# A decoder layer with expert retrieval: the attention projection in two passes of 128 tokens

## The chip, the core and the metric

The kernel runs on one core of one Trainium2 chip. The core has five engines that run side by side, each with its own queue of instructions: PE (TensorE, matrix products), DVE (VectorE), ACT (ScalarE), POOL (GpSimd) and SP (SyncE, which here only issues transfers). The engines order their work by semaphores. Transfers are carried out by 16 DMA engines. The metric is the device time of one execution in microseconds (us).

## What is computed

256 tokens of width 1024 go through two sub-layers, all in float32. The reference, cut:

```python
def token_mixer(h, ...):
    ...
    attn = nsa_attention(...)            # 16 heads, (256, 1024)
    y_a = attn @ w_attn_out
    y_b = conformer_conv(glu_in, ...) @ w_conv_out
    g_a, g_b = jnp.split(g_merge, 2, axis=-1)
    y = jax.nn.sigmoid(g_a) * y_a + jax.nn.sigmoid(g_b) * y_b
    return y @ w_out

def peer_ffn(h, w_q, sub_keys, u, v):
    q = (hf @ w_q).reshape(T, PEER_HEADS, 2, PEER_DQ // 2)     # 8 heads
    s = jnp.einsum('thcd,hckd->thck', q, sub_keys)
    s1, i1 = lax.top_k(s[:, :, 0], 16); s2, i2 = lax.top_k(s[:, :, 1], 16)
    # the best 16 of the 256 sums of pairs: 16 experts per token and head
    ...
        act = jax.nn.gelu(jnp.einsum('cd,ced->ce', hc, u[ec]))
        coef = act * wc
        return jnp.einsum('ce,ced->cd', coef, v[ec])
```

Between the two sub-layers stand a norm of the output, the residual sum and another norm (adaLN-conditioned); after the second one more norm and residual sum.

## The kernel before

**Stages.** Modulation and input projection (until about 250 us), the compressed, selected and window attention head by head (until 375 us), then the stages that the change touches, and from about 440 us the experts. Channels are in tiles of 128 (DT = 8 of them), tokens in TT = 2 halves of 128, called t = 0 and t = 1.

**Weights.** 103 tiles of 512 KB (128 x 1024) come in one order, `w_stream`. SP loads tile n into the place `SLOT[n]` of `ring`, eight places, when the tile that was there before (`PRIOR[n]`) is used up (semaphore `ring_used`, L367). T_AO (tiles 71 to 78) are the attention projection, T_OUT (79 to 86) the output projection, T_WQ (87 to 102) the query projection of the experts, one tile for each of 16 half heads.

**From attention to experts.** PE runs eight `column_tile`s of T_AO over all 256 tokens (L664), each of 8 products of 128x128 by 128x256; DVE multiplies each by its gate and adds the convolution branch into `y` (L1187, L1188, semaphore `v_m`). Then PE runs `out_part(0, k)` for the first tokens' output projection (L726), four of the eight `out_part(1, k)`, `h2_transposes(0)`, the first two query columns and their scores, the other four `out_part(1, k)`, two more query columns and `h2_transposes(1)`. A product of float32 shows as two MATMUL records of PE.
`out_norm(t)` and `ffn_norm(t)` on ACT and `token_norms(t)` on DVE make h2, the input of the experts, which `h2_transposes` and `h2_out` turn into h2T.

**Queries and scores.** `STEPS` lists which half head is projected for which tokens: 20 steps, the first eight for 128 tokens each. `query_columns(i)` and `subkey_scores(i)` run on PE, `query_out` and `score_out` on ACT. The first EARLY = 10 steps stand ahead of the experts; the other ten run between the chunks, one for every two.

**Retrieval.** `retrieve(k, part)` on DVE (three parts) finds for one head and 128 tokens the 16 experts, and gives their indices (`v_idx`). There are 16 units; each covers four chunks. Units 0 and 1 are done ahead of chunk 0, unit k + 2 in the course of unit k.

**Gathers.** POOL fetches for each n of 256 one row of 8 KB (u and v of an expert) for each of 128 tokens, 1 MB, into buffer `PLACE[n]` (L441 to L457). It waits first for all merges (`v_m`), then for the indices of each unit, and for a few buffers for their former content (`OUT_FREE`, `QUERY_FREE`). Twelve buffers are used until gather LATE = 92, from then on 16. Gather n waits until PE has used the row that was in its buffer (`p_row_used`). Four buffers are pairs of ring places; six are the arena.

**Chunks.** A chunk is four rows: DVE takes the dot product of each u with h2 (L1303), ACT the gelu, DVE multiplies by the softmax weight (`cf`), ACT writes four diagonal matrices (L926), and PE adds diagonal times v into PSUM (L697, 16 MATMUL records of 512 columns for a chunk). 64 chunks, 32 for each half of the tokens. `softmax_sum(k)` on DVE needs the exponential of unit k (`unit_exp`, ACT), with which goes a load of ACT's table, and another for the gelu behind it.

## Time and profile before

| | us |
|---|---|
| median of three runs | 1116.71 |
| lowest, highest | 1113.67, 1119.34 |
| profiled execution, its own time | 1119.28 |
| its span, first to last instruction | 1117.5 |
| busy in the span: PE / DVE / ACT / POOL | 966.3 / 728.0 / 280.1 / 328.3 |
| moved by DMA | 363.46 MB |
| of it gathers and other transfers of POOL (software queue) | 292.59 MB |
| mean granted clock of TensorE | 0.949 of 2.4 GHz |

The page's slices are each one fortieth of the span, 27.9 us; a digit is the busy share in tenths. In the rows below, times count from the start of the span. An entry such as "[3.65 <-ACT sig L926]" says that the engine was idle for 3.65 us before, and what ended it. Where a row is for several instructions (x16), its time is that from the first one's start to the last one's end.

### The profile page before, as it was taken

To read this page: it belongs to the slowest core of one execution; us is meant where nothing else is said; L and a number is where in the kernel's file an instruction comes from. 1 tells how busy PE (TensorE), PEld (TensorE's weight loads), DVE (VectorE), ACT (ScalarE), POOL (GpSimd) and SP (SyncE) were. 2 spreads that over 40 slices of the span, in tenths; PEclk is the share of its full clock that TensorE was granted. 3 is DMA by queue.
4 is the path that set the end of the run, shared out by engine and by line. 5 is a ranking of instruction groups with operands and counts; after the bars stand their busy time and mean duration, and the time that the engine had idled before them with its cause. 6 is when DMAs were issued, how large, how long until landed. Compare 5 with 4: busy or idle time off the path is not lost.

```text
span 1117.5 us, 10659 instructions
## 1 busy us (share of the span) xinstructions
PE 966.3 (86%) x3151; PEld 572.7 (51%) x3151; DVE 728.0 (65%) x1901; ACT 280.1 (25%) x770; POOL 328.3 (29%) x324
## 2 busy tenths in 40 slices
PE   5999999998999998899898987878768677878776
PEld 4888888776544765655454543333323233323332
DVE  6698997714455116686676676777677668667553
ACT  2111122143456102413212212221241221221212
POOL 0101002030000001355343445445434444445410
PEclk9999999997899999899899998989999999999988
DMA  9967649883101525999999999999999999999991
GB/s 364 403 245 242 230 154 398 337 237 80 38 20 36 176 90 169 419 422 420 424 421 424 422 423 423 422 422 424 422 423 424 422 423 423 423 422 423 424 422 71
DMA packets 63559, 363.46 MB, mean 325 GB/s; under 512 B 7515, under 2 KB 8171, under 8 KB 30476
## 3 DMA queue, kind: packets, MB, share of 16 engines
q0 software_dynamic: 43136, 292.59, 64.2%
q1 hardware_dynamic: 20364, 70.18, 17.2%
q8 instruction: 26, 0.43, 0.2%
q14 instruction: 33, 0.27, 0.1%
HBM read 361.15 MB, written 1.59 MB: 325 GB/s over the span
## 4 chain that ended last, share of the span: by engine, by line
PE 53%; DMA 35%; DVE 6%; ACT 2%; POOL 2%; issue 2%; SPq 0%; ACTq 0%; DVEq 0%; POOLq 0%
DMA pair<-in_peer_uv,idx 28%; PE pb L484 23%; PE pb L697 16%; DMA ring<-in_peer_uv,idx 4%; PE pb L499 3%; PE pb L635 2%; DMA arena<-in_peer_uv,idx 2%; PE pb L606 2%; PE pb L515 1%; PE pb L676 1%; DVE pair L1303 1%; PE pb L722 1%; PE pb L630 1%; POOL hT L454 1%; PE pb L588 1%
## 5 line engine op out<-in xcount | busy, mean ns | idle before, releaser
L697 PE MATMUL pb<-arena,sig 128*128 128x512 f32 x432 | 212.3, 645 | 63.2 <-ACT sig L926 63.0
L454 POOL DMA_INDIRECT arena<-in_peer_uv,idx x108 | 127.5, 1180 | 234.3 <-PE pb L697 164.6
L484 PE MATMUL pb<-hT,ring 128*128 128x256 f32 x880 | 190.7, 379 | 0.5 <-ACT arena L781 0.5
L484 PEld LDWEIGHTS pb<-hT,ring 128*128 128x128 f32 x880 | 167.0, 190 | 25.1 <-ACT arena L781 1.7
L1303 DVE CUSTOM_DVE_ANT_0 arena<-arena,sig 128x1024 f32<-128x1024 f32 x108 | 130.9, 1227 | 74.2 <-DMA arena<-in_peer_uv,idx 73.5
L697 PEld LDWEIGHTS pb<-arena,sig 128*128 128x128 f32 x432 | 86.4, 206 | 179.7 <-issue 179.4
L923 ACT ACTIVATE gl<-dot 128x4 f32<-128x4 f32 (+1 forms) x67 | 13.7, 205 | 443.9 <-DVE dot L1303 419.4
L697 PE MATMUL pb<-ring,sig 128*128 128x512 f32 x224 | 106.1, 618 | 21.2 <-ACT sig L926 21.2
L1050 DVE SCALAR_TENSOR_TENSOR y<-arena,cols,y x240 | 95.2, 473 | 0.0
L1303 DVE CUSTOM_DVE_ANT_0 ring<-ring,sig 128x1024 f32<-128x1024 f32 x56 | 67.8, 1224 | 29.8 <-DMA ring<-in_peer_uv,idx 29.4
L926 ACT ACTIVATE sig<-ident,cf 128x128 f32<-128x128 f32 x256 | 82.1, 390 | 15.4 <-DVE cf L1307 15.4
L697 PEld LDWEIGHTS pb<-ring,sig 128*128 128x128 f32 x224 | 43.6, 198 | 80.7 <-issue 80.7
L454 POOL DMA_INDIRECT ring<-in_peer_uv,idx x56 | 60.3, 1076 | 65.6 <-PE pb L697 51.7
L697 PE MATMUL pb<-qk,sig 128*128 128x512 f32 x156 | 75.5, 619 | 0.0
L697 PE MATMUL pb<-spare,sig 128*128 128x512 f32 x68 | 43.1, 767 | 32.4 <-ACT sig L926 32.4
L414 POOL DMA_DIRECT2D arena<-in_w_ada x32 | 17.1, 541 | 167.1 <-DVE modst L999 129.4
L1303 DVE CUSTOM_DVE_ANT_0 qk<-qk,sig 128x1024 f32<-128x1024 f32 x39 | 47.8, 1226 | 25.8 <-DMA qk<-in_peer_uv,idx 25.8
L697 PEld LDWEIGHTS pb<-qk,sig 128*128 128x128 f32 x156 | 32.1, 206 | 43.2 <-issue 43.2
L454 POOL DMA_INDIRECT qk<-in_peer_uv,idx x39 | 45.4, 1164 | 20.9 <-PE pb L697 14.8
L999 DVE CUSTOM_DVE_ANT_0 arena<-arena,sc 128x1024 f32<-128x1024 f32 x32 | 37.8, 1222 | 9.1 <-DMA arena<-in_w_ada 8.5
L484 PE MATMUL pb<-qk,ring 128*128 128x256 f32 x192 | 43.4, 379 | 0.0
L484 PEld LDWEIGHTS pb<-qk,ring 128*128 128x128 f32 x192 | 36.3, 190 | 9.1 <-issue 4.8
(226 smaller groups left out, 1220.5 us busy)
## 6 DMA issues: line engine op xcount, KB each, us to landing
ring<-in_w_stream SPq DMA_DIRECT2D x103, 512.0 KB, 6.8
arena<-in_w_ada POOLq DMA_DIRECT2D x32, 512.0 KB, 11.4
arena<-in_w_ada SPq DMA_DIRECT2D x12, 512.0 KB, 13.3
arena<-in_w1k SPq DMA_DIRECT2D x8, 512.0 KB, 8.8
sig<-in_w_ada SPq DMA_DIRECT2D x4, 512.0 KB, 15.3
arena<-in_w1v POOLq DMA_DIRECT2D x1, 2048.0 KB, 7.9
arena<-rev_scratch POOLq DMA_DIRECT2D x16, 128.0 KB, 6.6
arena<-in_peer_uv,idx POOLq DMA_INDIRECT x108, 26.7
```

Of the source, the lines that this page charges most:

```text
L414: g.dma_start(adaw[:, k, :], a["w_ada"][i * 8 + k]).then_inc(ada_more[k], 16)
L454: nc.gpsimd.indirect_dma_start(out=rowat[PLACE[n]], out_offset=None, in_=a["peer_uv"], in_offset=bass.IndirectOffsetOnAxis(ap=idx[:, c, e: ...
L484: last = mm(pb[:, bank, 0:SEQ], w[:, k * P:(k + 1) * P], src[:, k, :], start=(k == 0), stop=(k == DT - 1))
L499: last = mm(pb[:, n, 0:SEQ], ring[:, k, n * P:(n + 1) * P], hT[:, k, :], start=(k == 0), stop=(k == DT - 1))
L606: mm(pb[:, n % 2, 0:2 * keys], qT[0:DQK, h, tt * P:(tt + 1) * P], kT[0:DQK, g, 1:3, 0:keys], start=True, stop=True).then_inc(p_s, 1)
L635: last = mm(o, V[:, kb, (b * GROUPS + g) * DV:(b * GROUPS + g + 1) * DV], PT[:, gi % 2, b * (tt + 1) + kb, :], start=False, stop=((b, kb) ...
L697: last = mm(pb[:, 4 + 2 * t + hf, :], diag[:, c % DEEP, e, :], rowat[PLACE[n]][:, D + hf * 512:D + (hf + 1) * 512], start=(i == 0 and e == ...
L923: fn(gl[:, b, lo:hi], dot[:, b, lo:hi], ACT.Gelu_apprx_tanh).then_inc(a_gl, 1)
L926: fn(diag[:, b, s, :], ident[:, :], ACT.Copy, scale=cf[:, b, s:s + 1]).then_inc(a_dg, 1)
L999: V_.tensor_tensor_reduce(out=w[:, s, :], in0=w[:, s, :], in1=cact, scale=1.0, scalar=0.0, op0=ALU.mult, op1=ALU.add, accum_out=modst[:, s ...
L1050: ins = V_.scalar_tensor_tensor(out=y[:, j, :], in0=upad[:, j, k:k + SEQ], scalar=w, in1=y[:, j, :], op0=ALU.mult, op1=ALU.add)
L1303: V_.tensor_tensor_reduce(out=u, in0=u, in1=h2[:, c // CPT, :], scale=1.0, scalar=0.0, op0=ALU.mult, op1=ALU.add, accum_out=dot[:, c % DEE ...
```

## The change

The attention projection is done in two passes, one for each 128 tokens. The first pass, the first tokens' output projection and then four tiles of the second pass follow one another on PE; the other four tiles of the second pass stand behind the first two queries and scores, and the whole output projection of the second tokens behind them. The merges on DVE are split likewise: eight, then `token_norms(0)`, four, `retrieve(0)`, four, `token_norms(1)`. The second retrieval moves behind the dots of chunk 0.

The tiles of the output and query projections get places of their own outside the ring (`tile_at`): eight in the arena, six in spare, qk, V and y. The gather buffers are reordered: the ring and hT come first, then the arena. The first gather waits for `ring_used` to reach T_OUT (second pass used up), gather 5 for all merges, gather 7 for the output projection, gather 11 for the norms. LATE is 84, and the load of rows[3] stands there. h2 and the diagonals change places in `sig`. STEPS has 22 entries: six half heads for the first tokens, then by turns two for the second tokens and two for all; EARLY is 7, and from chunk 0 on there is one step for each chunk.

```diff
-SOON, SLOTS, LATE = 12, 16, 92
-OUT_FREE, QUERY_FREE = 10, 11
-STEPS = [(m, (0,)) for m in range(4)] + [(m, (1,)) for m in range(4)] + [(m, (0, 1)) for m in range(4, 2 * PH)]
+SOON, SLOTS, LATE = 12, 16, 84
+MERGED_FREE, OUT_FREE, NORM_FREE = 5, 7, 11
+STEPS = [(m, (0,)) for m in range(6)]
+for _m in (0, 2, 4):
+    STEPS += [(_m, (1,)), (_m + 1, (1,)), (_m + 6, (0, 1)), (_m + 7, (0, 1))]
+STEPS += [(m, (0, 1)) for m in range(12, 2 * PH)]
-EARLY = 10
+WQ_ORDER = [m for m, ts in STEPS if TT - 1 in ts]
+EARLY = 7
...
-        s = n % RING if m < 0 else (7, 0, 1, 2, 3, 6)[m] if m < 6 else (7, 0, 1, 6)[(m - 6) % 4]
+        s = n % RING if n < T_OUT else RING + n - T_OUT if m < 0 else RING + DT + m % 6
...
+OUT_BANK = (2, 6)
+MERGE_BANK = [0, 1, 4, 5] * 3 + [4, 5] * 2
+MERGE_BANK_BEFORE = [max((q for q in range(n) if MERGE_BANK[q] == MERGE_BANK[n]), default=-1) for n in range(TT * DT)]
...
+        rowat = [ring[:, 2 * i:2 * i + 2, :].rearrange("p a b -> p (a b)") for i in range(4)]
+        rowat += [hT[:, :, :].rearrange("p a b -> p (a b)")]
+        rowat += [arena[:, 2 * i:2 * i + 2, :].rearrange("p a b -> p (a b)") for i in range(6)]
+        rowat += [pair[:, :]]
+        rowat += [spare[:, :], qk[:, 3 * D:5 * D], qk[:, 5 * D:7 * D], qk[:, 0:2 * D]]
+        tile_at = [ring[:, i, :] for i in range(RING)]
+        tile_at += [arena[:, i, :] for i in (8, 9, 10, 11, 4, 5, 6, 7)]
+        tile_at += [spare[:, 0:D], spare[:, D:2 * D], qk[:, 3 * D:4 * D], qk[:, 4 * D:5 * D],
+                    V[:, :, :].rearrange("p a b -> p (a b)"), yf[:, D:2 * D]]
...
# SP
-                sp.wait_ge(ring_used, PRIOR[n] + 1)
-                sp.dma_start(ring[:, SLOT[n], :], a["w_stream"][n]).then_inc(ring_in[SLOT[n]], 16)
+                if PRIOR[n] >= 0:
+                    sp.wait_ge(ring_used, used(PRIOR[n]))
+                if n == T_OUT:
+                    sp.wait_ge(v_mx, 2 * NU)
+                if n == T_OUT + 4:
+                    sp.wait_ge(p_o, GROUPS * TT)
+                if n == T_WQ + 5:
+                    sp.wait_ge(ring_used, T_WQ)
+                sp.dma_start(tile_at[SLOT[n]], a["w_stream"][n]).then_inc(ring_in[SLOT[n]], 16)
...
# POOL
-            g.wait_ge(v_mx, 2 * NU)
-            g.wait_ge(v_m, DT)
+            g.wait_ge(ring_used, T_OUT)
...
+                if n == MERGED_FREE:
+                    g.wait_ge(v_m, TT * DT)
                 if n == OUT_FREE:
                     g.wait_ge(ring_used, T_WQ)
-                if n == QUERY_FREE:
-                    g.wait_ge(ring_used, T_WQ + 5)
+                if n == NORM_FREE:
+                    g.wait_ge(v_h2, TT)
                 if n == LATE:
...
+                    rows_load(3)
...
# PE
+            def attention_out_half(t, j):
+                tile = T_AO + j
+                if t == 0:
+                    pe.wait_ge(ring_in[SLOT[tile]], 16 * TURN[tile])
+                if MERGE_BANK_BEFORE[t * DT + j] >= 0:
+                    pe.wait_ge(v_m, MERGE_BANK_BEFORE[t * DT + j] + 1)
+                for k in range(DT):
+                    last = mm(pb[:, MERGE_BANK[t * DT + j], 0:P], tile_at[SLOT[tile]][:, k * P:(k + 1) * P],
+                              hT[:, k, t * P:(t + 1) * P], start=(k == 0), stop=(k == DT - 1))
+                last.then_inc(ring_used if t else p_ao, 1)
...
             for k in range(DT):
                 last = out_part(0, k)
             last.then_inc(p_out, 1)
-            for k in range(4):
-                out_part(1, k).then_inc(ring_used, 1)
+            pe.wait_ge(a_o, 2 * GROUPS * TT)
+            for j in range(4):
+                attention_out_half(1, j)
             h2_transposes(0)
-            pe.wait_ge(a_h2T, 2)
             pe.wait_ge(sub_in, 16)
+            pe.wait_ge(v_m, DT + 2)
             query_columns(0)
             query_columns(1)
             subkey_scores(0)
             subkey_scores(1)
-            for k in range(4, DT):
+            for j in range(4, DT):
+                attention_out_half(1, j)
+            for k in range(DT):
                 out_part(1, k).then_inc(ring_used, 1)
-            query_columns(2)
-            query_columns(3)
-            subkey_scores(2)
-            subkey_scores(3)
+            for i in range(2, 6):
+                query_columns(i)
+                if i > 2:
+                    subkey_scores(i - 1)
+            subkey_scores(5)
             h2_transposes(1)
             pe.wait_ge(a_h2T, 4)
-            for i in range(4, EARLY):
+            for i in range(6, EARLY):
                 query_columns(i)
-                if i > 4:
-                    subkey_scores(i - 1)
-            subkey_scores(EARLY - 1)
+                subkey_scores(i)
             for c in range(TT * CPT):
                 expert_chunk(c)
-                i = EARLY + c // 2
...
+                if 0 < c and EARLY + c - 1 < len(STEPS):
+                    subkey_scores(EARLY + c - 1)
+                if EARLY + c < len(STEPS):
+                    query_columns(EARLY + c)
...
# ACT, ahead of the chunks
             out_norm(1)
             query_out(2)
+            query_out(3)
             ffn_norm(1)
-            query_out(3)
+            unit_exp(0)
+            gelu_next()
             score_out(2)
+            query_out(4)
             score_out(3)
+            query_out(5)
+            score_out(4)
+            score_out(5)
             h2_out(1)
...
# DVE
             for part in range(3):
                 retrieve(0, part)
+            for j in range(4, DT):
+                merged(1, j)
             token_norms(1)
-            for part in range(3):
-                retrieve(1, part)
             for c in range(TT * CPT):
...
+                if c == 0:
+                    for part in range(3):
+                        retrieve(1, part)
```

## Rows read from the trace of the kernel before

**Rows 1.** The page, DMA busy tenths and GB/s in 40 slices.
```profile
DMA  9967649883101525999999999999999999999991
GB/s 364 403 245 242 230 154 398 337 237 80 38 20 36 176 90 169 419 422 420 424 421 424 422 423 423 422 422 424 422 423 424 422 423 423 423 422 423 424 422 71
```

**Rows 2.** Stretches: length, busy us of each engine, PEclk, DMA share, GB/s.
```profile
440.00:450.00 10.00, 5.38 (x30) 4.60 (x29) 9.27 (x27) 3.25 (x8) 7.52 (x7) 0.74 0.79 287
...
900.00:1080.00 180.00, 136.34 (x281) 56.31 (x281) 119.04 (x286) 38.62 (x106) 80.80 (x70) 0.92 1.01 423
...
1092.00:1100.00 8.00, 5.98 (x7) 2.50 (x8) 4.79 (x10) 2.69 (x9) 0.00 (x0) 0.58 0.17 72
```

**Rows 3.** Timeline of DVE, the last three dots: start, us, instruction, idle before.
```profile
1096.64 1.23 DVE L1303 CUSTOM_DVE_ANT_0 ring<-ring,sig 128x1024 f32<-128x1024 f32 x1 [0.47 <-DMA ring<-in_peer_uv,idx]
...
1099.10 1.23 DVE L1303 CUSTOM_DVE_ANT_0 qk<-qk,sig 128x1024 f32<-128x1024 f32 x1 [0.81 <-DMA qk<-in_peer_uv,idx]
...
1101.56 1.23 DVE L1303 CUSTOM_DVE_ANT_0 qk<-qk,sig 128x1024 f32<-128x1024 f32 x1 [0.80 <-DMA qk<-in_peer_uv,idx]
```

**Rows 4.** Timeline of POOL: the load of rows[3], gathers 0 and 12.
```profile
375.73 0.53 POOL L436 DMA_DIRECT2D V<-rows_scratch  x1 [3.59 <-PE pb L635]
440.66 1.00 POOL L454 DMA_INDIRECT arena<-in_peer_uv,idx  x1 [64.40 <-DVE idx L1256]
...
473.98 0.94 POOL L454 DMA_INDIRECT arena<-in_peer_uv,idx  x1 [11.33 <-PE pb L697]
```

**Rows 5.** Timeline of PE from the attention projection to chunk 3.
```profile
375.36 27.89 PE L484 MATMUL pb<-hT,ring 128*128 128x256 f32 x128
403.09 20.76 PE L676 MATMUL pb<-ring,y 128*128 128x512 f32 x48
424.16 1.09 PE L685 MATMUL pb<-ident,sig 128*128 128x128 f32 x8 [0.31 <-DVE sig L1207]
...
430.52 7.03 PE L676 MATMUL pb<-ring,y 128*128 128x512 f32 x16
...
469.95 9.83 PE L697 MATMUL pb<-arena,sig 128*128 128x512 f32 x16 [3.65 <-ACT sig L926]
...
500.71 7.03 PE L697 MATMUL pb<-arena,sig 128*128 128x512 f32 x16
```

**Rows 6.** Chain of work that ended last: one query tile for 128 tokens.
```profile
453.96 1.79 PE pb L722 x16
```

**Rows 7.** Timeline of DVE: a merge, the first retrieval's start and end, two dots.
```profile
379.19 0.42 DVE L1187 TENSOR_TENSOR pair<-pb,sig 128x256 f32<-128x256 f32 x1 [7.87 <-PE pb L484]
...
431.13 0.48 DVE L1217 MAX8 v<-sc 128x8 f32<-128x128 f32 x2 [7.02 <-ACT sc L931]
...
439.59 0.17 DVE L1256 SCALAR_TENSOR_TENSOR idx<-e 128x16 int32<-128x16 f32 x1
...
465.42 1.22 DVE L1303 CUSTOM_DVE_ANT_0 arena<-arena,sig 128x1024 f32<-128x1024 f32 x1
...
466.57 1.22 DVE L1303 CUSTOM_DVE_ANT_0 arena<-arena,sig 128x1024 f32<-128x1024 f32 x1
```

**Rows 8.** Weight loads issued in 412:440, 441:470, 449:452, 455:460, us to landing.
```profile
ring<-in_w_stream SPq DMA_DIRECT2D x6, 512.0 KB, 3.8
ring<-in_w_stream SPq DMA_DIRECT2D x4, 512.0 KB, 9.3
ring<-in_w_stream SPq DMA_DIRECT2D x1, 512.0 KB, 8.1
ring<-in_w_stream SPq DMA_DIRECT2D x1, 512.0 KB, 11.8
```

**Rows 9.** Timeline of ACT: from the exponential's table load to the gelu's.
```profile
462.05 1.28 ACT L912 ACT_TABLE_LOAD   x1
...
464.87 0.20 ACT L915 ACTIVATE turned<-eps 128x1 f32<-128x1 f32 x1
```

**Rows 10.** Timeline of PE: scores of one step for 256 tokens.
```profile
489.94 0.61 PE L709 MATMUL pb<-qk 128*128 128x128 f32 x4
```

More of the change, by code:

```diff
@@ L126, with used @@
 SLOT, TURN, PRIOR = tile_places()
+def used(n):
+    return n + 1 if n < T_WQ else T_WQ + 1 + WQ_ORDER.index(n - T_WQ)
+OUT_BANK = (2, 6)
+MERGE_BANK = [0, 1, 4, 5] * 3 + [4, 5] * 2
+MERGE_BANK_BEFORE = [max((q for q in range(n) if MERGE_BANK[q] == MERGE_BANK[n]), default=-1) for n in range(TT * DT)]
 def landed(n):
@@ L294, in build @@
                                                   ("x_in", "c_in", "cols_in", "table_in", "onehot_in", "small_in"))
-        ring_in = [sem(f"ring_in{i}") for i in range(RING)]
+        ring_in = [sem(f"ring_in{i}") for i in range(RING + DT + 6)]
+        p_ao = sem("p_ao")
         ada_in = [sem(f"ada_in{i}") for i in range(2 * DT)]
@@ L472, in _ @@
                     last.then_inc(p_xT, 1)
-            def attention_landed(k):
-                return 2 * (GROUPS * TT - 1) + (2 if k >= DT - 2 else 0)
             def column_tile(bank, tile, src, ready=None, count=lambda k: k + 1):
-                w = ring[:, SLOT[tile], :]
+                w = tile_at[SLOT[tile]]
                 pe.wait_ge(ring_in[SLOT[tile]], 16 * TURN[tile])
@@ L708, in subkey_scores @@
                 for t in ts:
-                    last = mm(pb[:, 2 + i % 2, t * NK:(t + 1) * NK], query[:, m % 4, t * P:(t + 1) * P],
+                    last = mm(pb[:, 2 + i % 2, t * NK:(t + 1) * NK], query[:, i % 4, t * P:(t + 1) * P],
                               subk[:, m, :], start=True, stop=True)
@@ L721, in query_columns @@
                 for k in range(DT):
-                    last = mm(pb[:, i % 2, 0:P], ring[:, SLOT[T_WQ + m], k * P:(k + 1) * P],
+                    if k % 4 == 0:
+                        pe.wait_ge(a_h2T, 2 * ts[0] + k // 4 + 1)
+                    last = mm(pb[:, i % 2, 0:P], tile_at[SLOT[T_WQ + m]][:, k * P:(k + 1) * P],
                               h2T[:, k, ts[0] * P:(ts[0] + 1) * P], start=(k == 0), stop=(k == DT - 1))
                 last.then_inc(ring_used if ts[0] else p_q, 1)
+            pe.wait_ge(a_pt, NU)
             for k in range(DT):
@@ L940, in query_out @@
                 else:
-                    act.wait_ge(ring_used, T_WQ + m + 1)
-                fn(query[:, m % 4, ts[0] * P:(ts[-1] + 1) * P], pb[:, i % 2, 0:len(ts) * P], ACT.Copy).then_inc(a_q, 1)
+                    act.wait_ge(ring_used, used(T_WQ + m))
+                fn(query[:, i % 4, ts[0] * P:(ts[-1] + 1) * P], pb[:, i % 2, 0:len(ts) * P], ACT.Copy).then_inc(a_q, 1)
             out_norm(0)
@@ L1209, in token_norms @@
                 dve.wait_ge(v_h2, t + 1)
-            dve.wait_ge(rows_in, 64)
+            dve.wait_ge(rows_in, 48)
             token_norms(0)
+            for j in range(4):
+                merged(1, j)
             def top16(n_rows, src, work, vals, idxs):
@@ L1232, in retrieve @@
                 t, q = divmod(k, CPT // SEG)
+                swork, cand, cwork, oneh = (v[min(k, 1)] for v in (sworks, cands, cworks, onehs))
                 pair = v16[:, :, :].rearrange("p (h c) k -> p h c k", c=2)
```

105 lines of the change are left out of this document (48 added, 57 removed).

## The prediction, made before the changed kernel was run

> **What bounds the kernel now.** I read first the page's line of DMA by slices, because one resource must explain the second half: from slice 16 on, some 447 us, to slice 39 it shows nines and 420 to 425 GB/s without a gap [rows 1]. The stretches agree: 423 GB/s at a share of 1.01 from 900 us to 1080 us, while PE is busy for only 136 of those 180 us [rows 2]. So from the first row gather on, the kernel moves 256 gathers of 1 MB each (128 rows of 8 KB), plus what weights are left, at one fixed rate; one gather costs 2.48 us of it (1.049 MB at 423 GB/s), which is also the spacing of the last dot products, 1096.64 and 1099.10 [rows 3]. What ends last is then the last landing plus a tail of some 16 us.
>
> Hence the time is set by three things: **when the gathers begin**, **how many bytes are left to move then**, and **whether the DMA runs dry later**. Only these three count below. The stretch 440 to 450 moved 2.87 MB, 6.8 us of full rate, so full rate began at 443.2, 2.5 us after the issue of the first gather at 440.66 [rows 2, 4]. A gather n needs its buffer: the first 12 have free ones, each later one waits until PE has used the row 12 places earlier. In the kernel before that margin is thin but holds: the first 12 gathers (29.8 us) and the four weight tiles issued between 441 and 470 (4 x 1.24 us) last until 478.0, and the 13th is issued at 473.98, so its data flow at 476.5 [rows 4, 8]. Chunk 0 of the experts starts on PE at 469.95 [rows 5].
>
> **Part 1: the first tokens' path gets shorter.** Before, PE does the attention projection of all 256 tokens from 375.36 in 27.89 us, 3.49 a tile, then the first tokens' output projection, 32 records of 0.4325 us (20.76/48), until 416.9 [rows 5]. A tile for 128 tokens should cost what a query column tile of 128 tokens costs: 1.79 us [rows 6]. So the first pass takes 8 x 1.79 = 14.3 us and ends at 389.7, and the first output projection (13.84 us) at 403.5: 13.4 us earlier. Its merges on DVE (two operations of 0.42 us at 256 tokens, less at 128) [rows 7] and the weights, for which SP now has free places as soon as the scores end, lie under PE. A tile landed in 3.8 us while the DMA was idle [rows 8], and the last of these 8 is needed at 401.8. The norms to h2 take as before 7.2 us (416.93 to 424.12) [rows 5], until 410.7; the four tiles of the second pass that PE does meanwhile are 4 x 1.79 = 7.2 us, as long, so they cost nothing. Transposes, first two queries and scores: retrieval started 7.0 us after h2 (424.12 to 431.13) [rows 5, 7]; the wait on half of h2T saves 0.4 us, thus 417.3. Retrieval takes 8.6 us (431.13 to 439.76) [rows 7]: **the first indices are there at 426.0, 13.8 us earlier.**
>
> **Part 2: but the gathers don't start then.** POOL now waits until all of the second pass is used (its first buffers are the ring). Tiles 4 and 5 run at 416.9 to 420.5, but tile 6 needs the bank of tile 4, whose merge stands on DVE behind the whole first retrieval: it comes at 426.8. PE is idle for 6.3 us. In this trace an idle PE loses its clock: after 3.65 us idle, 16 records took 9.83 us where 7.03 is usual, and in 440 to 450 the granted clock is 0.74 on average, that is partly at 1.2 GHz [rows 2, 5]. Tiles 6 and 7 therefore take between 3.6 and 7.2 us and end between 430.4 and 434.0. I take 433.0, since the low stretch after 469.95 lasted 6 us (2.9 us were lost at half speed). With 0.4 us to the issue, gather 0 is issued at 433.4 instead of 440.66: **-7.3 us** (ends -6.3 and -9.9). The second output projection, which frees buffers 7 to 10, is queued behind these tiles: it ends at 446.9, where before it ended at 437.5 [rows 5]. That is later, but seven gathers (17.4 us) cover until 453.3.
>
> **Part 3: bytes left.** Before, 6 query tiles were in by the first gather and 10 of 16 were left; now 5 are in (the sixth waits for y), so one tile more: +1.24 us. The broadcast of rows[3], 0.5 MB, was done at 375.73 on an idle DMA [rows 4]; now POOL issues it ahead of gather 84: +1.2 us. Together **+2.5 us**. The DMA rate stays; that the gathers' buffers lie elsewhere costs nothing that a row shows, between -1 and +1 us.
>
> **Part 4: does the DMA run dry?** This term decides. The chain to chunk 0: after 446.9 PE needs the sixth query tile, which is requested only then, behind seven gathers. Such a load landed 8.1 to 11.8 us after its issue when gathers were queued [rows 8], so at 455.0 to 458.7, and PE has nothing else from 453 on. I take 456.5, the lower end, as fewer gathers are queued. Then the query itself (1.8 to 3.6 us, again after an idle PE), two scores, the 8 transposes, the evacuation behind two score evacuations on ACT, and one more query with its score give some 6 us more, and chunk 0 starts on PE at 464.7, after its first row the 13th gather's data flow at 468.6. The two table loads with the exponential between (462.05 to 464.87) [rows 9] now stand ahead of score 2 on ACT, from 453 to 456, under the same wait. The DMA has work from 435.9 for 29.8 us and two tiles, until 468.2: **0.4 us dry**.
>
> Next, the second retrieval (8.6 us) has moved behind chunk 0's dots. DVE does it, then four dots (1.15 us each [rows 7]), then come gelu, coefficient and diagonals (1.1 us): chunk 1 starts 13.9 us after chunk 0, and as PE had been idle for 5 us, its first row takes 3.4 us and not 1.7. From row to row that is 15.6 us, in which the DMA has 4 gathers and a tile, 11.2 us: **4.4 us dry**. Then PE is the pace: a chunk is 6.9 us (16 x 0.4325), and there is one step of query and score with each chunk instead of every other: 3.5 us for 256 tokens, 1.79 for 128, 0.4 for the score [rows 6, 10]. 10.8 us against the DMA's 9.9: chunk 2 adds 2.0 us (the rest of the slow clock in it), chunk 3 0.9. From chunk 4 the steps are short ones and two more tiles are to be loaded; the margin grows back. Sum 7.7 us; from it I take 1 us, since not all 16 DMA engines are equally far, and those behind still have work. **+6.7 us** (ends +2 with a fast clock and an early tile, +12 with a tile at 458.7).
>
> That some engines lag can be seen at the end: 1092 to 1100 shows a share of 0.17, yet DVE still waits for landings until 1101.5 [rows 2, 3]. So the last landing is set by the slowest engine. In the Trainium skill, DMA: Bandwidth & Descriptors (Latency and other measured facts), two of the engines are called usually slower under descriptors from GpSimd; by it the lag would grow evenly over the gathers, and in the first 16 of them would be well under a microsecond, so the sum stays.
>
> The same page (Queues, rings and completion order) says that each engine takes turns between queues packet by packet. By it the sixth query tile would move at about half the rate, some 4.5 us, and not wait for the gathers ahead; chunk 0 would start some 2 us earlier and the sum would be about 0. The trace's 8.1 to 11.8 us speak against it, so I stay with the rows.
>
> **The sum.** -7.3 + 2.5 + 6.7 = +1.9 us. The profiled execution took 1119.28 us at a span of 1117.5, 2.6 above the median of the three runs, 1116.71, which lie between 1113.67 and 1119.34; the difference goes on the median: **1118.5 us**. About 0.5% (5.6 us) is what a measurement can tell from no change.
>
> **The rivals.**
> (A) The early start is kept: the sixth query tile lands early, PE keeps 2.4 GHz and the dry spells are covered. For it: the margin before held with the same 12 buffers, and the DMA is never seen dry. Against: the second retrieval after chunk 0 is 8.6 us that no other work of DVE hides. It gives -7.3 + 2.5 = -4.8, to -7.4 with the earlier end of the second pass: 1109.3 to 1111.9, about 1110.5. Chance 0.22.
> (B) Slower: the sixth query tile. Requested at 446.9 behind seven gathers, it decides from about 457 on: every microsecond later delays chunk 0, with it gather 12, and as the DMA has only 12 buffers' work, the end, one for one. At 458.7 PE has been idle for 5.7 us, the query takes 3.6 us, chunk 0 starts at about 469 and the 13th gather flows at 473: 5 us dry there, 12 in all. -7.3 + 2.5 + 12 = +7.2: 1124. For it: the 11.8 us seen; against: the backlog is shorter here. Chance 0.22.
> (C) The change doesn't move the start: if the wait for the merges and the slow clock push the end of the second pass 3 us beyond its worst end, gathers start at 437 or later, and -3.7 + 2.5 + 6.7 = +5.5: 1122 or more. Chance 0.06.
> The forecast, 1114 to 1121.5, has 0.50.
>
> **The numbers.** Faster by over 0.5% (under 1111.1): most of A and a little of the forecast's lower tail, 0.22. Slower (over 1122.3): B and C, 0.25. Within: 0.53. For 8 in 10 the range must reach into both: 1109.5 to 1126.
>
> **What would show it.** First gather issued at 433 to 434, 7 us earlier, and the first indices at 426; PE idle between about 420.5 and 426.8, the second output projection ending near 447; PE waiting for the weights of the sixth query near 453 to 456; chunk 0 at about 465; DMA slices below full rate between 465 and 510 us, 5 to 8 us in sum; from there to the end 423 GB/s and the tail unchanged. Were the DMA full from 436 us on, A is right. Were it dry beyond chunk 4, the pace of one step to a chunk was costed too low. I would be wrong altogether if the rate of the gathers changed with their new places or a stall showed after gather 84.

## The result

| | before | changed |
|---|---|---|
| median, us | 1115.72 (20 runs) | 1119.51 (20 runs) |
| lowest to highest, us | 1110.68 to 1121.10 | 1114.50 to 1122.92 |
| profiled execution, its span, us | 1119.28, 1117.5 | 1117.12, 1115.4 |

The ratio is 1.0031, with a 95% interval of 1.0016 to 1.0046: about 3.5 us slower, within the 0.5% that was called no change. The two profiled executions stand the other way round, by 2.1 us. That comes mainly from ahead of the change: the attention projection begins at 375.36 in the one [rows 5] and at 370.92 in the other. It varies from one execution to the next: in x11 below, which does the same work up to there as the kernel before, it begins at 371.44. So everything below is counted **from the start of the attention projection**, and by that the last landing comes 3.5 us later in the changed kernel. From the last dot product's start to the end of the span it takes 15.9 us in the one and 14.8 in the other; -4.4 + 3.5 - 1.2 makes the -2.1. What this tail depends on stands in the last section.

The page of the changed kernel, DMA busy tenths and GB/s in 40 slices, which answer to [rows 1]:

```profile
DMA  9967649884102705989999999999999999999992
GB/s 368 403 236 241 238 153 379 333 256 89 38 20 78 300 1 207 389 331 401 422 422 422 422 423 422 422 424 421 423 423 422 423 424 422 422 423 423 422 423 123
```

The slices 12 to 15, counted from 0, have changed (78, 300, 1, 207 GB/s: the weights come early, then nothing, then the gathers), and the slices at full rate are no longer without a gap: 389, 331 and 401 GB/s stand in slices 16 to 18, from 446 to 530 us. The stretches (length, busy us of each engine, PEclk, DMA share, GB/s), as [rows 2]:

```profile
430.00:440.00 10.00, 10.00 (x24) 4.37 (x24) 0.19 (x1) 0.00 (x0) 6.07 (x7) 1.00 0.87 315
...
460.00:470.00 10.00, 8.73 (x30) 4.75 (x31) 8.47 (x36) 3.05 (x9) 3.66 (x4) 1.00 0.91 342
470.00:480.00 10.00, 5.05 (x12) 2.44 (x12) 9.59 (x28) 3.26 (x9) 0.06 (x1) 0.66 0.82 330
480.00:490.00 10.00, 10.00 (x35) 6.00 (x34) 9.56 (x24) 2.15 (x7) 4.57 (x4) 1.00 0.82 319
490.00:500.00 10.00, 10.00 (x36) 6.24 (x35) 8.83 (x24) 2.42 (x9) 4.06 (x4) 1.00 0.95 346
500.00:510.00 10.00, 10.00 (x40) 5.69 (x39) 5.93 (x17) 6.07 (x15) 5.25 (x4) 1.00 0.98 368
510.00:520.00 10.00, 10.00 (x38) 5.46 (x38) 6.23 (x16) 0.74 (x3) 4.87 (x5) 1.00 1.01 422
...
900.00:1080.00 180.00, 139.61 (x287) 57.53 (x286) 120.04 (x287) 38.62 (x106) 82.06 (x70) 0.92 1.01 423
```

Between 460 and 510 us the DMA moves 342, 330, 319, 346 and 368 GB/s instead of 422. Ten us at each come to 0.80 + 0.92 + 1.03 + 0.76 + 0.54 MB too little: **4.1 MB, or 9.6 us at full rate**. 6.2 us of it lie ahead of 482.6 (351 GB/s from 460 to 466, 330 to 470, 385 to 474, 56 from 478 to 482.6, 2.5 us after the issue of the 17th gather), 3.4 us behind. Afterwards all is as before.

The timeline of PE, which answers to [rows 5]: start, us, instructions, idle before.

```profile
370.92 14.56 PE L693 MATMUL pb<-hT,ring 128*128 128x128 f32 x128
385.31 13.90 PE L713 MATMUL pb<-arena,y 128*128 128x512 f32 x32
...
412.33 3.74 PE L693 MATMUL pb<-hT,ring 128*128 128x128 f32 x32
422.37 6.75 PE L693 MATMUL pb<-hT,ring 128*128 128x128 f32 x32 [6.30 <-DVE y L1230]
428.95 13.90 PE L713 MATMUL pb<-arena,y 128*128 128x512 f32 x32
...
451.79 3.22 PE L759 MATMUL pb<-qk,y 128*128 128x128 f32 x16 [3.14 <-ACT qk L980]
...
461.75 7.10 PE L732 MATMUL pb<-ring,sig 128*128 128x512 f32 x16 [1.18 <-ACT sig L964]
...
475.60 3.75 PE L732 MATMUL pb<-hT,sig 128*128 128x512 f32 x4 [4.95 <-ACT sig L964]
...
488.25 5.31 PE L732 MATMUL pb<-arena,sig 128*128 128x512 f32 x12
...
499.01 7.03 PE L732 MATMUL pb<-ring,sig 128*128 128x512 f32 x16
```

To be seen here: the first pass in 14.4 us where all 256 tokens took 27.89 [rows 5]; 6.30 us without work ahead of tiles 6 and 7, which then take 6.75 us for 3.6 us of work; 3.14 us idle ahead of the sixth query; chunk 0 at 461.75; and 4.95 us idle ahead of chunk 1. For the sixth query the row names ACT, whose evacuation of the fifth ends at 451.75. But in the kernel `query_columns(5)` waits only for the fourth evacuation, done by 446.7, and for its weights: issued at 442.88, they landed 8.8 us later, at 451.7. The timeline of POOL, gathers 0, 12 and 16, which answers to [rows 4]:

```profile
429.40 1.01 POOL L484 DMA_INDIRECT ring<-in_peer_uv,idx  x1 [61.70 <-PE pb L693]
...
463.98 0.93 POOL L484 DMA_INDIRECT ring<-in_peer_uv,idx  x1 [12.82 <-PE pb L732]
...
480.12 0.93 POOL L484 DMA_INDIRECT hT<-in_peer_uv,idx  x1 [10.06 <-PE pb L732]
```

And DVE: the first indices; the second norms, which stand behind 13.91 us of idle time; and the last dot.

```profile
421.40 0.18 DVE L1302 SCALAR_TENSOR_TENSOR idx<-e 128x16 int32<-128x16 f32 x1
...
444.10 1.23 DVE L1238 TENSOR_TENSOR sc<-pb,sc 128x1024 f32<-128x1024 f32 x1 [13.91 <-ACT pair L930]
```

```profile
1100.62 1.23 DVE L1350 CUSTOM_DVE_ANT_0 arena<-arena,sig 128x1024 f32<-128x1024 f32 x1 [0.80 <-DMA arena<-in_peer_uv,idx]
```

### The profile page after: what moved, and what is told of

It reads as the page before. It is cut to its first block, busy times and chain, and to the rows that moved or that the text cites. A ratio compares the mean times of both kernels' runs of the same rounds, so it can differ in the third digit from the quotient of the medians.

```text
span 1115.4 us, 11016 instructions
## 1 busy us (share of the span) xinstructions
PE 962.1 (86%) x3311; PEld 575.9 (52%) x3311; DVE 730.9 (66%) x1917; ACT 280.9 (25%) x774; POOL 329.9 (30%) x324
## 4 chain that ended last, share of the span: by engine, by line
PE 51%; DMA 35%; DVE 6%; ACT 2%; SPq 2%; POOL 2%; issue 2%; ACTq 0%; DVEq 0%; POOLq 0%
DMA ring<-in_peer_uv,idx 29%; PE pb L511 20%; PE pb L732 16%; DMA pair<-in_peer_uv,idx 4%; PE pb L693 3%; PE pb L713 2%; PE pb L662 2%; PE pb L633 2%; DMA arena<-in_w_ada 2%; PE pb L759 1%; DVE ring L1350 1%; DMA arena<-in_w1k 1%; POOL ring L484 1%; PE pb L657 1%; PE pb L615 1%
## 5 line engine op out<-in xcount | busy, mean ns | idle before, releaser
L732 PE MATMUL pb<-ring,sig 128*128 128x512 f32 x288 | 143.6, 657 | 32.5 <-ACT sig L964 32.5
L511 PE MATMUL pb<-hT,ring 128*128 128x256 f32 x752 | 162.8, 379 | 0.5 <-ACT arena L819 0.5
L511 PEld LDWEIGHTS pb<-hT,ring 128*128 128x128 f32 x752 | 142.7, 190 | 21.1 <-ACT arena L819 1.7
L484 POOL DMA_INDIRECT ring<-in_peer_uv,idx x72 | 82.5, 1146 | 170.1 <-PE pb L732 102.3
L961 ACT ACTIVATE gl<-dot 128x4 f32<-128x4 f32 (+1 forms) x67 | 13.7, 205 | 425.1 <-DVE dot L1350 425.1
L732 PEld LDWEIGHTS pb<-ring,sig 128*128 128x128 f32 x288 | 59.2, 210 | 113.2 <-issue 113.1
L1350 DVE CUSTOM_DVE_ANT_0 ring<-ring,sig 128x1024 f32<-128x1024 f32 x72 | 87.1, 1228 | 41.2 <-DMA ring<-in_peer_uv,idx 40.7
L1088 DVE SCALAR_TENSOR_TENSOR y<-arena,cols,y x240 | 95.2, 476 | 0.0
L732 PE MATMUL pb<-qk,sig 128*128 128x512 f32 x132 | 59.4, 600 | 0.0
L732 PE MATMUL pb<-hT,sig 128*128 128x512 f32 x72 | 36.6, 632 | 22.9 <-ACT sig L964 22.9
L732 PE MATMUL pb<-spare,sig 128*128 128x512 f32 x44 | 23.8, 666 | 20.5 <-ACT sig L964 20.5
L885 ACT ACTIVATE pair<-pair,nm 128x128 f32<-128x128 f32 (+1 forms) x64 | 28.5, 447 | 40.2 <-DVE nm L1179 40.1
## 6 DMA issues: line engine op xcount, KB each, us to landing
arena<-in_w_ada SPq DMA_DIRECT2D x12, 512.0 KB, 13.4
qk<-in_w_stream SPq DMA_DIRECT2D x6, 512.0 KB, 13.4
```

The lines of the kernel that those rows point to most:

```text
L484: nc.gpsimd.indirect_dma_start(out=rowat[PLACE[n]], out_offset=None, in_=a["peer_uv"], in_offset=bass.IndirectOffsetOnAxis(ap=idx[:, c, e: ...
L511: last = mm(pb[:, bank, 0:SEQ], w[:, k * P:(k + 1) * P], src[:, k, :], start=(k == 0), stop=(k == DT - 1))
L732: last = mm(pb[:, 4 + 2 * t + hf, :], diag[:, c % DEEP, e, :], rowat[PLACE[n]][:, D + hf * 512:D + (hf + 1) * 512], start=(i == 0 and e == ...
L885: fn(S[:, n % 4, b, 0:keys], S[:, n % 4, b, 0:keys], ACT.Exp, scale=-1.0, bias=nm[:, n % 2, b:b + 1], accum_out=Z[:, n % 2, b:b + 1]).then ...
L1088: ins = V_.scalar_tensor_tensor(out=y[:, j, :], in0=upad[:, j, k:k + SEQ], scalar=w, in1=y[:, j, :], op0=ALU.mult, op1=ALU.add)
L1350: V_.tensor_tensor_reduce(out=u, in0=u, in1=h2[:, c // CPT, :], scale=1.0, scalar=0.0, op0=ALU.mult, op1=ALU.add, accum_out=dot[:, c % DEE ...
```

## The experiments

Each kernel was timed against the kernel before in five rounds. All compute the full result. The table counts from the start of the attention projection (in brackets the us in the trace at which that is); "13th" is the issue of the first gather that reuses a buffer, "17th" that of the first one that needs a row of chunk 1, and "last dot" the start of the last dot product, which is the last landing. Three kernels have a buffer more (x4, x8, x11); for them it is the 14th and the 18th gather. x2 and x4 start their gathers 1 us ahead of the changed kernel with the same code up to there: tiles 6 and 7 took 5.76 and 5.82 us in them, behind the same 6.3 us of idle time, where the changed kernel's trace has 6.75. So differences of 1 us in the table are no more than one execution differs from the next.

| kernel | first gather | 13th | 17th | last dot | 17th to last dot | ratio to before, 95% |
|---|---|---|---|---|---|---|
| before (375.36) | 65.3 | 98.6 | 110.4 | 726.2 | 615.8 | 1 |
| changed (370.92) | 58.5 | 93.1 | 109.2 | 729.7 | 620.5 | 1.0031 (1.0016 to 1.0046) |
| x1 retrieval ahead of chunk 0 (371.97) | 58.5 | 100.1 | 110.4 | 731.6 | 621.3 | 1.0037 (1.0019 to 1.0056) |
| x2 sixth tile's own place (372.04) | 57.5 | 88.6 | 104.5 | 724.5 | 620.0 | 0.9993 (0.9973 to 1.0014) |
| x3 more banks (370.62) | 51.5 | 87.9 | 104.1 | 724.4 | 620.4 | 0.9980 (0.9956 to 1.0004) |
| x4 thirteen buffers (373.78) | 57.5 | 94.0 | 109.6 | 726.7 | 617.1 | 1.0003 (0.9980 to 1.0025) |
| x5 idle time used (373.75) | 57.2 | 96.8 | 106.0 | 727.4 | 621.4 | 1.0007 (0.9983 to 1.0030) |
| x6 x5 and x3 (371.41) | 51.5 | 93.5 | 102.6 | 723.7 | 621.1 | 0.9976 (0.9952 to 0.9999) |
| x7 x6 and x2 (371.04) | 51.5 | 86.0 | 95.2 | 716.5 | 621.4 | 0.9912 (0.9880 to 0.9943) |
| x8 x6, thirteen buffers (373.17) | 51.5 | 93.5 | 102.1 | 720.1 | 618.0 | 0.9943 (0.9922 to 0.9963) |
| x9 x5, one line on ACT (374.59) | 57.2 | 91.8 | 101.0 | 722.1 | 621.2 | 0.9958 (0.9939 to 0.9977) |
| x10 x6, one line on ACT (371.67) | 51.5 | 87.8 | 97.0 | 718.0 | 621.0 | 0.9930 (0.9903 to 0.9958) |
| x11 before, thirteen buffers (371.44) | 65.3 | 98.6 | | 725.6 | | 1.0001 (0.9982 to 1.0020) |
| x12 x7 with EARLY 6 (373.87) | 51.5 | 85.0 | 95.0 | 716.7 | 621.7 | 0.9909 (0.9876 to 0.9942) |

The theory was that the end follows the moment at which the first chunks free their buffers, because the DMA runs dry until then; the rivals were that the gathers' start decides, or the bytes and the new places. **The sixth column carries the answer**: in the changed kernel and its nine relatives with twelve buffers, the last landing comes 620.0 to 621.7 us after the issue of the 17th gather, while the first gather's issue varies by 7 us and the 17th's by 15. And the last dot agrees with the time: for each of the thirteen kernels its distance from that of the kernel before is the one that the ratio gives, within 1.4 us.

The column is to be read with care. The 17th gather was picked from the table, after the runs; taken from the 18th, 19th or 20th, the interval spreads by 1.9, 2.2 and 1.7 us, from the 13th by 6.4 and from the first by 8.2. Nor is the queue in the same state at that moment. In the changed kernel, x2 and x3 it is empty then, and the DMA falls short by another 5 us or so behind it. In the seven others the DMA is short ahead of the 17th gather and full from then on, since the four gathers ahead of it were issued 9 to 10 us earlier at the most, not 16, and part of them is still in the queue: in the 36 us behind the issue x7 moves 15.2 MB and the changed kernel 12.9. That both kinds come out at 620 to 622 us is what ten traces show, and no rule that these runs explain.

### x1: the second retrieval ahead of chunk 0

```diff
             token_norms(1)
+            for part in range(3):
+                retrieve(1, part)
...
-                if c == 0:
-                    for part in range(3):
-                        retrieve(1, part)
```

> The changed kernel with one part undone: the second retrieval stands again ahead of chunk 0. My theory (the DMA runs dry for want of freed buffers, most of all while chunk 1 waits for this retrieval): chunk 0 starts 3.4 us later, as its dots wait for the retrieval, but chunk 1 follows it at once, its first row about 3.7 us earlier than in the changed kernel; the shortfall of the DMA between 460 and 510 us falls from about 10 us to about 6, and the time by some 4 us, to the kernel before within 0.1%: ratio to before 0.999 to 1.000. Rival (the order of retrieval is hidden, what costs are bytes and the new places): chunk 0 later by 3.4 us and nothing gained, ratio 1.003 to 1.006.

Nothing was gained: 1.0037. PE:

```profile
468.08 9.97 PE L732 MATMUL pb<-ring,sig 128*128 128x512 f32 x16 [6.24 <-ACT sig L964]
477.89 1.95 PE L759 MATMUL pb<-qk,spare 128*128 128x128 f32 x16
479.68 1.88 PE L732 MATMUL pb<-hT,sig 128*128 128x512 f32 x4
```

Chunk 1 did follow at once, and its rows came 1.2 us later all the same (17th gather 110.4 against 109.2). The 3.4 us of delay that I had reckoned for chunk 0 were 5.3, as seen from the start of the projection (96.1 against 90.8), PE was idle for 6.24 us ahead of it, and chunk 0 took 9.97 us, not 7.10. The idle time had only moved from ahead of chunk 1 to ahead of chunk 0. In this kernel the retrieval's place is worth nothing so long as PE must wait for it somewhere; this speaks neither for my expectation nor for the rival, which had the time right but for a reason (the order is hidden) that this trace doesn't show.

### x2: a place of its own for the sixth query tile

```diff
-                    V[:, :, :].rearrange("p a b -> p (a b)"), yf[:, D:2 * D]]
+                    V[:, :, :].rearrange("p a b -> p (a b)"), extra[:, :]]
...
-                if n == T_WQ + 5:
-                    sp.wait_ge(ring_used, T_WQ)
```

> The changed kernel, but the sixth query tile has 4 KB of its own per partition and is loaded with the other five, so nothing waits for it. My theory: PE doesn't wait 3.1 us for it, keeps its clock, chunk 0 starts about 4 us earlier and every later row of the first chunks with it; the end comes about 4 us earlier, ratio to before 0.999 to 1.001, with the gathers' start unchanged. Rival (the start of the gathers decides): no change against the changed kernel, ratio 1.003.

As expected: 0.9993, against 1.0031. The gathers start where they did, give or take 1 us, but the sixth query follows without a pause, and the 13th and 17th gather are issued 4.4 and 4.7 us earlier. PE and POOL:

```profile
448.61 1.95 PE L758 MATMUL pb<-qk,extra 128*128 128x128 f32 x16
...
458.44 7.10 PE L731 MATMUL pb<-ring,sig 128*128 128x512 f32 x16 [1.18 <-ACT sig L963]
```

```profile
429.52 1.00 POOL L483 DMA_INDIRECT ring<-in_peer_uv,idx  x1 [60.71 <-PE pb L692]
...
460.67 0.94 POOL L483 DMA_INDIRECT ring<-in_peer_uv,idx  x1 [9.38 <-PE pb L731]
...
476.52 1.15 POOL L483 DMA_INDIRECT hT<-in_peer_uv,idx  x1 [9.76 <-PE pb L731]
```

### x3: more banks, so that the gathers start 7 us earlier

```diff
-MERGE_BANK = [0, 1, 4, 5] * 3 + [4, 5] * 2
+MERGE_BANK = [0, 1, 4, 5] * 3 + [4, 5, 6, 7]
...
-                pe.wait_ge(v_m, t * DT + k + 1)
+                pe.wait_ge(v_m, TT * DT if t else k + 1)
```

> The changed kernel, but tiles 6 and 7 of the second pass have PSUM banks of their own (6, 7), so PE doesn't wait for merges behind the first retrieval; the second output projection then waits for all merges. Rival theory (the start of the gathers decides): they start about 7 us earlier, at 0.9 us after the first indices, and the time falls by 7 us, ratio to before 0.996 to 0.997. My theory: the rows of the first chunks free buffers hardly earlier (the output projection ends some 2.5 us earlier), so the earlier start is given back as a longer dry spell of the DMA, and the time falls by only 2 to 3 us, ratio 1.000 to 1.001.

The ratio, 0.9980, lies between the two. The trace decides:

```profile
422.13 1.00 POOL L484 DMA_INDIRECT ring<-in_peer_uv,idx  x1 [54.74 <-DVE idx L1302]
...
458.55 0.94 POOL L484 DMA_INDIRECT ring<-in_peer_uv,idx  x1 [9.39 <-PE pb L732]
...
474.69 0.94 POOL L484 DMA_INDIRECT hT<-in_peer_uv,idx  x1 [10.06 <-PE pb L732]
```

The start moved by 7.0 us (51.5 against 58.5), the 17th gather by 5.1 and the last landing by 5.3. So the end went with the 17th gather. That moved by more than the 2.5 us I had given it. The second output projection ended only 1.7 us earlier (70.1 for 71.8; behind 4.78 us of idle time it took some 16.6 us instead of 13.7). But the sixth tile, issued at 440.88, landed 4.5 us later, ahead of 446.49, when PE came to it, so PE didn't wait for it and chunk 0 started at 85.7 for 90.8. So x3 tests the start only together with an early tile; the comparison with x2 parts the two. x2, with the old start, has the same end (724.5 and 724.4).

```profile
y<-in_w_stream SPq DMA_DIRECT2D x1, 512.0 KB, 4.5
```

### x4: a thirteenth buffer

```diff
-SOON, SLOTS, LATE = 12, 16, 84
+SOON, SLOTS, LATE = 13, 17, 84
...
+        extra = sb("extra", [P, 2 * D])
-        rowat += [pair[:, :]]
+        rowat += [pair[:, :], extra[:, :]]
```

> The changed kernel with a thirteenth gather buffer from the first gather on (17 instead of 16 at the end), in 8 KB per partition that were free. Same order of work on every engine. My theory (freed buffers limit the DMA): the DMA has 2.48 us more work in hand, the shortfall between 460 and 510 us falls by that, the end comes 2 to 3 us earlier, ratio to before 1.000 to 1.002, and chunk 0 starts at the same time as in the changed kernel. Rival (the DMA falls short for another reason, such as the rate of the gathers in their new places): no change, ratio 1.003.

As expected: 1.0003 and a last landing 3.0 us earlier, with PE's work in the same order and chunk 0 at the same place but for 0.9 us (91.8 against 90.8). The buffer itself accounts for 2.48 us of that, one gather's time. POOL:

```profile
453.39 1.18 POOL L485 DMA_INDIRECT extra<-in_peer_uv,idx  x1 [0.30 <-issue]
467.78 0.94 POOL L485 DMA_INDIRECT ring<-in_peer_uv,idx  x1 [13.20 <-PE pb L733]
```

### x11: the same buffer in the kernel before

```diff
-SOON, SLOTS, LATE = 12, 16, 92
+SOON, SLOTS, LATE = 13, 17, 92
...
-        rowat += [qk[:, 3 * D:5 * D], ring_rows[2], ring_rows[1], ring_rows[0], ring_rows[3]]
+        rowat += [qk[:, 3 * D:5 * D], ring_rows[2], ring_rows[1], extra[:, :], ring_rows[0], ring_rows[3]]
```

> The kernel before, with a thirteenth gather buffer. Its DMA shows no dry spell, so my theory expects nothing from it: ratio to before 0.999 to 1.001, where the same buffer gave the changed kernel 3 us. Rival (one buffer more is worth 3 us in any of them): 0.997 to 0.998.

1.0001: where the DMA never runs dry, a buffer more gives nothing. x4 and x11 together show that the buffer is worth something only where there is a dry spell.

### x5 and x9: using the idle time

```diff
# PE: behind the first two scores
-            for j in range(4, DT):
-                attention_out_half(1, j)
+            attention_out_half(1, 4)
+            attention_out_half(1, 5)
+            query_columns(2)
+            query_columns(3)
+            subkey_scores(2)
+            subkey_scores(3)
+            attention_out_half(1, 6)
+            attention_out_half(1, 7)
...
# DVE: behind the merges, with a scratch in pair[:, 0:D]
+            for part in range(3):
+                retrieve(1, part)
             token_norms(1)
...
# ACT
+            query_out(2)
+            query_out(3)
+            score_out(2)
+            score_out(3)
             out_norm(1)
+            query_out(4)
+            query_out(5)
             ffn_norm(1)
```

> The changed kernel, but queries and scores 2 and 3 run on PE between tiles 5 and 6 of the second pass, where it was idle for 6.3 us, and the second retrieval (on a scratch of its own, in pair) on DVE ahead of the second norms, where it was idle for 14 us. Same work otherwise. My theory (the end follows the moment at which the first chunks free their buffers): tiles 6 and 7 keep the fast clock, gathers start 3 us earlier, chunk 0 some 3 us earlier, and chunk 1 follows it at once, its first row 10 us earlier than in the changed kernel; the DMA's shortfall between 460 and 510 us falls from about 10 us to about 2; the time by 9 to 11 us, ratio to before 0.993 to 0.995. Rival (as in the run with the retrieval ahead of chunk 0, its place is of no use; only the 3 us of the start count): ratio 1.000 to 1.001.

1.0007, far from the 0.993 to 0.995 expected. ACT and PE say why:

```profile
456.28 0.28 ACT L985 ACTIVATE qk<-pb 128x128 f32<-128x128 f32 x1 [9.78 <-PE pb L759]
456.45 1.05 ACT L942 ACTIVATE pair<-x 128x1024 f32<-128x1024 f32 x1
```

```profile
452.49 3.75 PE L759 MATMUL pb<-qk,y 128*128 128x128 f32 x16 [6.31 <-issue]
...
459.56 1.51 PE L720 MATMUL pb<-ident,sig 128*128 128x128 f32 x8 [2.45 <-DVE sig L1255]
...
468.34 1.95 PE L732 MATMUL pb<-ring,sig 128*128 128x512 f32 x4 [1.18 <-ACT sig L969]
```

I had put the evacuation of query 5 ahead of the second norm's square (L942). That query waits for the late sixth tile, so ACT stood for 9.78 us, and with it the second norms, h2T, gather 11 and chunk 0 (94.6 for 90.8). x9 moves this one line:

```diff
             query_out(4)
-            query_out(5)
             ffn_norm(1)
             unit_exp(0)
             gelu_next()
+            query_out(5)
             score_out(4)
```

> The kernel with queries 2, 3 and the second retrieval in the idle time, with one line moved on ACT: the evacuation of query 5, which waits for the late sixth tile, stands behind the second norm's square and the table loads, no longer ahead of them. My theory: in the run before, that evacuation held up the second norm for 10 us, so chunk 0 came 3.7 us later than in the changed kernel (each counted from the start of its attention projection); without it chunk 0 comes 5 to 6 us earlier than there and the end with it, ratio to before 0.995 to 0.997. Rival (chunk 0 doesn't matter, the place of the retrieval is of no use): as before, 1.000 to 1.001.

0.9958, as expected. The last landing comes 5.3 us earlier than in x5, the 17th gather 5.0. The 17th gather comes 8.2 us earlier than in the changed kernel, and the last landing 7.6. x9 differs from it in the retrieval's place and in that of two queries; PE's rows part the two:

```profile
464.15 7.11 PE L732 MATMUL pb<-ring,sig 128*128 128x512 f32 x16 [1.18 <-ACT sig L969]
...
472.88 1.88 PE L732 MATMUL pb<-hT,sig 128*128 128x512 f32 x4
```

Chunk 0 comes 1.3 us earlier (89.6 for 90.8), but chunk 1 follows 8.7 us behind it and not 13.9, and its first row takes 1.88 us and not 3.75. So most of the gain is the retrieval's: its place is worth its time after all, if it lies where no engine waits for it.

### x6, x8 and x10: with the banks of x3

x6 is x5 with the banks of x3 (all four tiles first, then the two queries). x10 moves the line on ACT, x8 is x6 with a thirteenth buffer.

> The kernel with queries and retrieval in the idle time, and banks 6 and 7 for tiles 6 and 7 as well, so that the gathers start right behind the first indices. My theory: now that the first chunks are early too, the earlier start counts in full: gathers start 7 us before those of the changed kernel, chunk 0 some 6 us earlier, the DMA short by at most 2 us, the time 13 to 16 us less than the changed kernel, ratio to before 0.989 to 0.991. Rival (the start counts for nothing, only the chunks do): the same as without the banks, 0.993 to 0.995.

> The kernel with idle time used and more banks, and with a thirteenth gather buffer. Where the changed kernel gained 3 us from it, my theory expects at most 1 to 2 us here, since the DMA hardly runs dry any more: ratio to before 0.988 to 0.991. Rival (a buffer more is worth 3 us whatever the rest): 3 us less than without it.

> The same line moved in the kernel that has banks 6 and 7 besides. My theory: chunk 0 some 5 us earlier, the shortfall of the DMA between 450 and 480 us down by as much, ratio to before 0.992 to 0.994, still behind the version with the tile in a place of its own (0.991), since the tile still lands after 446 us. Rival: 0.9976 as without.

x6 gave 0.9976 instead of 0.989 to 0.991, for the reason of x5; x10 0.9930, in the range expected. From x9 to x10 the 17th gather moves by 4.0 us, the last landing by 4.1 and the first gather by 5.7. x8 gave 0.9943 instead of 0.988 to 0.991. Against x6 it gained 3.6 us by the last landing, not 1 to 2: my number had rested on a DMA that no longer ran dry, and in x6 it did (273 and 154 GB/s between 450 and 470 us). For the case that it did, the theory asks for 2.48 us; what the other 1.1 us are isn't shown.

### x7 and x12: all of it

x7 is x6 with the sixth tile's own place (x2). With that tile there, ACT doesn't wait.

> The same with the sixth query tile in a place of its own, loaded with the other five. My theory: chunk 0 starts another 3 to 4 us earlier, but there is hardly a dry spell left to close: 1 to 2 us for it and 1.2 us for the tile that is loaded while the DMA is idle; ratio to before 0.987 to 0.990. Rival (an earlier chunk 0 is always worth its time, as in the run with that change alone): 4 us less than without, 0.985 to 0.987.

**0.9912** (0.9880 to 0.9943, from 7 runs), a median of 1104.66 us: faster than both kernels, 11 us under the runs of the kernel before on the same chip. It lies above the 0.987 to 0.990 that I expected. POOL, and the stretch that is left:

```profile
422.57 1.01 POOL L483 DMA_INDIRECT ring<-in_peer_uv,idx  x1 [54.74 <-DVE idx L1304]
...
457.03 1.43 POOL L483 DMA_INDIRECT ring<-in_peer_uv,idx  x1 [9.50 <-PE pb L731]
...
466.19 1.31 POOL L483 DMA_INDIRECT hT<-in_peer_uv,idx  x1 [2.13 <-PE pb L731]
```

```profile
440.00:450.00 10.00, 5.65 (x35) 4.87 (x35) 8.70 (x14) 6.21 (x14) 3.76 (x4) 0.78 1.01 424
450.00:460.00 10.00, 8.45 (x28) 5.25 (x28) 7.29 (x19) 5.85 (x15) 2.37 (x2) 0.88 0.79 304
460.00:470.00 10.00, 10.00 (x37) 5.43 (x36) 9.45 (x33) 2.31 (x8) 5.94 (x5) 1.00 0.98 399
470.00:480.00 10.00, 10.00 (x34) 6.08 (x33) 9.16 (x21) 2.14 (x7) 3.43 (x5) 1.00 1.01 426
```

The DMA is still short by 2.8 and 0.5 us (304 and 399 against 422 GB/s). x12 was to take that away by starting chunk 0 ahead of a step:

```diff
-EARLY = 7
+EARLY = 6
```

> The kernel with idle time used, more banks and the sixth tile's own place, and with step 6 behind chunk 0 (EARLY 6), so that chunk 0 doesn't wait for its query, score and evacuations. Its shortfall between 450 and 470 us was 3.4 us. My theory: chunk 0 starts 2 us earlier and takes 1.5 to 2 us of it away, ratio to before 0.989 to 0.991. Rival (PE is the pace from chunk 0 on, a step moved behind it is paid there): no change, 0.991.

0.9909: no change against x7, as the rival had it, though not for its reason alone. The ratio lies in my range too and can't decide; the last landing does (716.7 for 716.5).

```profile
448.53 1.09 PE L719 MATMUL pb<-ident,sig 128*128 128x128 f32 x8 [2.74 <-DVE sig L1252]
454.81 9.78 PE L731 MATMUL pb<-ring,sig 128*128 128x512 f32 x16 [5.18 <-ACT sig L966]
464.43 1.95 PE L758 MATMUL pb<-qk,spare 128*128 128x128 f32 x16
```

Chunk 0 did start 2.8 us earlier (80.9 against 83.8). But PE had been idle for 5.18 us and did it in 9.78 us, where x7 took 7.11; the granted clock of 450 to 460 was 0.50. The 17th gather gained 0.2 us.

## Why the prediction was right

Point by point, each from the start of the projection (375.4 in the prediction's count), measured for predicted:

- **The first pass and the indices.** 14.4 us for 14.3; the first output projection at its end after 28.1 for 28.1; indices at 50.5 for 50.6 (421.40 - 370.92). Here the 13.4 us are gained in full.
- **The gathers' start.** The wait for the merges behind the first retrieval: 6.30 us for 6.3. Tiles 6 and 7 in 6.75, between the bounds of 3.6 and 7.2, ending at 58.0 for 57.6. First gather 6.8 us earlier for 7.3.
- **The sixth query tile.** The load landed 8.8 us after its issue (row below), at the lower end of the 8.1 to 11.8 taken from [rows 8]; PE went on at 80.9 for 81.1. The estimate of 4.5 us from the rule of turns between queues (the Trainium skill, DMA: Bandwidth & Descriptors, Queues, rings and completion order) is not what this load took. In x3 the tile did take 4.5 us, but there, at 2.48 us a gather from 424.6 on (an estimate: the first issue and 2.5 us), only some 1 us of the seven gathers was left ahead of it, so x3 can't tell turns from a wait behind them.
- **Chunks.** Chunk 0 at 90.8 for 89.3; chunk 1 13.9 us behind it for 13.9; chunk 2 at 117.3 for 116.8; chunk 3 at 128.1 for 127.6 (the last two predictions follow from its steps from row to row).
- **The shortfall.** This is the term that was mis-sized: 7.7 us predicted, 9.6 measured in bytes. Up to 2.5 us after the 17th gather's issue it was 6.2 us for 0.4 + 4.4; chunk 0 came 1.5 us later than reckoned. Behind that it was 3.4 us for 2.0 + 0.9. At the last landing the term is 3.5 + 6.8 - 2.5 = 7.8 us, where the sum had 6.7: of the shortfall 1.8 us didn't reach the last landing, for the 1 us that was taken off. That the lag of single DMA engines is the reason, as the prediction argues, no trace here shows.
- **Bytes.** 2.5 us for 2.5. From the issue of the first gather to the end the DMA moves 275.07 MB in the kernel before and 276.12 in the changed one (rows below, 440.66:1117.5 and 429.40:1115.4): 1.05 MB more, half of it on SP's queue (6.29 and 6.82 MB), half on POOL's (268.45 and 268.98). No stall or change of rate shows after gather 84 (423 GB/s from 900 to 1080).

The bytes, before and changed, and issue to landing of the load at 442.88 in the stretch 440 to 450 of the changed kernel:

```profile
DMA packets 38908, 275.07 MB, mean 406 GB/s; under 512 B 4320, under 2 KB 4320, under 8 KB 6112
DMA packets 39196, 276.12 MB, mean 403 GB/s; under 512 B 4352, under 2 KB 4352, under 8 KB 6400
...
y<-in_w_stream SPq DMA_DIRECT2D x1, 512.0 KB, 8.8
```

The sum was +1.9 us and the measurement says 3.5 (1.8 to 5.1). The rivals fell by the traces: (A) by the shortfall, (C) by the start at 429.40, and (B), the tile later than 457 (81.6 from the projection's start), by its landing at 80.8. That was close, and x2 shows that (B) had the right suspect: the wait for that tile was worth 4.2 us by the ratio even at the early end. What the forecast didn't see is that the gathers' start stands in its sum twice, with opposite signs: as the -7.3, and in the shortfall, since the DMA's work ends the earlier the earlier it began (435.9 + 29.8 us and two tiles). Once the DMA runs dry the start cancels out. x2 and x3 have starts 6 us apart and the same end (724.5 and 724.4). So the ends of -6.3 and -9.9 us that it gave for the start were no uncertainty of the time, except as far as the start moves the sixth tile.

## What to carry to other kernels

When a transfer queue is the bound and its buffers are handed back by other engines, an earlier start is only a loan: reckon when the first buffers come back, since in these kernels the end followed the gathers into those buffers and not the first gather. Ask of every step moved ahead of or behind the loop which engine is idle at its new place, since moving an idle gap from one chunk to another gained nothing (x1) and moving the work into idle time did (x9). And on an in-order engine put no evacuation that waits for a late load ahead of a norm that others wait for: one such line cost 5.3 us (x5 against x9) and 5.7 (x6 against x10).
